# One core, two transformer blocks in three-pass matmuls: row statistics by token, eight weight slots, all weight splits on GpSimd

## The reference, cut to what matters

```
h = x
h += rms(gmlp(rms(h)))                       # u * (W_s layernorm(v) + b), gelu
h += rms(relu(rms(h) @ up)**2 @ down)        # feed-forward 1, 4096 hidden
h += rms(band_attention(rms(h), rms(h)@wk, rms(h)@wv))   # 16 heads
h += rms(relu(rms(h) @ up)**2 @ down)        # feed-forward 2
h += 0.5 * (silu(rms(h) @ gate) * (rms(h) @ up)) @ down  # feed-forward 3, 2816 hidden
h += w_out(branch_a * sigmoid + branch_b * sigmoid)      # top-k attention, retention
h += 0.5 * swiglu(rms(h))                    # feed-forward 4
h += sigmoid(rms(h) @ g) * (p @ w)           # last projection
out = rms(h)
rms(x) = x * rsqrt(mean(x*x, last axis) + eps) * gain
```

## Time and profile before

| | |
|---|---|
| median of 3 runs | 2698.27 us (2697.91 to 2699.78) |
| the profiled execution | 2702.41 us, its span 2700.6 us |
| PE busy, mean granted clock | 2487.4 us (92%), 0.944 |
| DVE, ACT, POOL busy | 1434.4, 796.1, 518.7 us |
| the chain that ended last | PE 81%, DVE 14%, ACT 2% |
| low parts by DVE (L1128), by POOL (L319) | 292 and 119 units |

### The profile page before, as it was taken

The page is one execution under the profiler, slowest core; times in us unless marked ns, Lnnn a source line. Parts: engine busy times, 40 slices in busy tenths (PEclk is TensorE's granted clock), DMA queues, the critical chain, the costliest instruction groups (busy, mean ns, idle before and its releaser), DMA issues.

```text
span 2700.6 us, 30486 instructions
## 1 busy us (share of the span) xinstructions
PE 2487.4 (92%) x10766; PEld 1964.8 (73%) x10766; DVE 1434.4 (53%) x1974; ACT 796.1 (29%) x1226; POOL 518.7 (19%) x243
## 2 busy tenths in 40 slices
PE   6888999979998999996999997978989998999996
PEld 5666888856666788884888885555567887888875
DVE  4566434473666543457534466797434336444456
ACT  2134223331433332233323232312322113322233
POOL 6600000015432000000000005452026871000000
PEclk9889999989998999997999998986599999999998
DMA  4222333322222233321333332121012323333322
GB/s 165 70 78 63 94 101 94 93 71 85 84 62 63 86 94 100 94 82 55 109 95 100 95 88 75 48 77 32 0 43 74 100 87 94 101 96 99 88 76 70
DMA packets 64805, 221.52 MB, mean 82 GB/s; under 512 B 7504, under 2 KB 9680, under 8 KB 64592
## 3 DMA queue, kind: packets, MB, share of 16 engines
q1 hardware_dynamic: 59184, 208.17, 26.0%
q10 hardware_dynamic: 5536, 12.19, 1.4%
HBM read 218.23 MB, written 2.10 MB: 82 GB/s over the span
## 4 chain that ended last, share of the span: by engine, by line
PE 81%; DVE 14%; ACT 2%; issue 2%; ACTq 0%; POOL 0%; DVEq 0%; POOLq 0%
PE PS L368 23%; PE PS L370 22%; PE PS L369 22%; PE PS L438 3%; DVE RI L1158 1%; PE PS L498 1%; PE PS L519 1%; DVE SS L1140 1%; DVE MK L1494 1%; DVE TOP L1493 1%; DVE XL L1148 1%; PE PS L708 1%; PE PS L625 1%; PE PS L646 1%; PE PS L635 1%
## 5 line engine op out<-in xcount | busy, mean ns | idle before, releaser
L368 PE MATMUL PS<-XH,WH 128*128 128x512 f32 x1816 | 730.3, 402 | 80.8 <-DVE WL L1128 35.6
L369 PE MATMUL PS<-XL,WH 128*128 128x512 f32 x1816 | 715.8, 394 | 0.0
L370 PE MATMUL PS<-XH,WL 128*128 128x512 f32 x1816 | 715.4, 394 | 0.0
L316 POOL TENSOR_TENSOR WH<-RAW,ONES 128x1024 fp32r<-128x1024 f32 (+1 forms) x119 | 231.0, 1942 | 1709.5 <-PE PS L370 1157.5
L368 PEld LDWEIGHTS PS<-XH,WH 128*128 128x128 f32 x1816 | 347.3, 191 | 182.4 <-issue 69.0
L1128 DVE TENSOR_TENSOR WL<-RAW,WH 128x1024 fp32r<-128x1024 f32 (+2 forms) x292 | 346.9, 1188 | 202.3 <-ACT WH L797 194.0
L370 PEld LDWEIGHTS PS<-XH,WL 128*128 128x128 f32 x1816 | 346.2, 191 | 73.9
L369 PEld LDWEIGHTS PS<-XL,WH 128*128 128x128 f32 x1816 | 347.3, 191 | 70.8 <-issue 1.4
L797 ACT ACTIVATE WH<-RAW 128x1024 fp32r<-128x1024 f32 (+2 forms) x292 | 297.8, 1020 | 340.2 <-DVE M L1240 336.2
L368 PE MATMUL PS<-HH,WH 128*128 128x512 f32 x992 | 389.6, 393 | 3.0 <-DVE WL L1128 3.0
L370 PE MATMUL PS<-HH,WL 128*128 128x512 f32 x992 | 386.8, 390 | 0.0
(11 more groups left out here) (202 smaller groups left out, 2412.1 us busy)
## 6 DMA issues: line engine op xcount, KB each, us to landing
RAW<-in_weights SPq DMA_DIRECT2D x379, 512.0 KB, 3.5
RAW<-in_weights SPq DMA_DIRECT2D x16, 384.0 KB, 3.1
H<-in_xT ACTq DMA_DIRECT2D x8, 256.0 KB, 8.9
BIAS<-in_rel ACTq DMA_DIRECT2D x8, 256.0 KB, 3.5
RAW<-in_weights SPq DMA_DIRECT2D x8, 256.0 KB, 2.6
out<-R ACTq DMA_DIRECT2D x8, 256.0 KB, 2.2
BIAS<-in_rel ACTq DMA_DIRECT2D x8, 224.0 KB, 3.8
DECAY<-in_decay ACTq DMA_DIRECT2D x1, 1024.0 KB, 4.9
```

The source lines that it names most:

```text
L316: nc.gpsimd.tensor_tensor(WH[:, slot, 0:w], raw, ONES[:, 0:1].to_broadcast([P, w]), ALU.mult).then_inc(high_split, 1)
L368: nc.tensor.matmul(PS[:, bank_, :], WH[:, slot, w], xh[:, k, :], start=(k == 0), stop=False)
L369: nc.tensor.matmul(PS[:, bank_, :], WH[:, slot, w], xl[:, k, :], start=False, stop=False)
L370: return nc.tensor.matmul(PS[:, bank_, :], WL[:, slot, w], xh[:, k, :], start=False, stop=stop)
```

## The change

1. **Statistics by token** everywhere: `stat` makes four matmuls with one column (SS as the stationary side), so that each token's sum is one number on a partition; root and reciprocal are over 128x4. `spread` multiplies the reciprocal, broadcast along 128 columns, by the identity, four matmuls, and so puts it back in all rows, in bank 4 (read there by L1254 instead of RI) or in bank 5, from where ACT copies it into RI.
2. **Eight weight slots** in three ranges (WIDE: units 24 to 91, 120 to 255, 331 on): WH2/WL2 (and WHA, WLA where those are in use) beside WH/WL. RAW keeps four.
3. **Four units together** at the start of a feed-forward, and the unit after them (SPARE: 28, 124, 188, 331) goes into bank 7, so it waits for no evacuation.
4. **No memset** of M: the first down group copies, the later ones add. The `ffn` code is partly unrolled for it.
5. **The rotation tables** (sines, by DVE and ACT) move from the branch of ffn_a1 into the first down group of ffn_b1.
6. **POOL splits all units**; `split_high` and `split_low` do nothing any more.

```diff
-POOL_RANGES = ((0, FIRST["gmlp_out"] + 4), (FIRST["att_v"] + 4, FIRST["ffn_a1"]),
-               (FIRST["mix_heads"] + 4, FIRST["ffn_b2"]))
+POOL_RANGES = ((0, UNITS),)
+AHEAD = 8
+WIDE = ((24, 92, 20), (120, 256, 116), (331, UNITS, 328))
+SPARE = (28, 124, 188, 331)
+def weight_slot(u):
+    for first, end, zero in WIDE:
+        if first <= u < end:
+            return (u - zero) % (2 * SLOTS)
+    return u % SLOTS
+def slot_before(u):
+    return next((v for v in range(u - 1, max(-1, u - 3 * SLOTS), -1) if weight_slot(v) == weight_slot(u)
+                 and (weight_slot(u) < SLOTS or u - v == 2 * SLOTS)), None)
+def bank_of(u):
+    return 7 if u in SPARE else u % SLOTS
...
-        ANG = at("ANG", 32, [P, 3, SEQ])
+        ANG = at("ANG", 196, [P, 2, SEQ])
...
+        WH2 = at("WH2", 144, [P, SLOTS, UNIT], F32R)
+        WL2 = at("WL2", 160, [P, SLOTS, UNIT], F32R)
+        WLA = at("WLA", 80, [P, SLOTS, UNIT], F32R)
+        WHA = at("WHA", 188, [P, 3, UNIT], F32R)
...
+        def weights_of(u):
+            k = weight_slot(u)
+            if k < SLOTS:
+                return WH[:, k, :], WL[:, k, :]
+            high = WHA[:, k - SLOTS, :] if 331 < u < 335 else WH2[:, k - SLOTS, :]
+            low = WLA[:, k - SLOTS, :] if 120 <= u < 124 else WL2[:, k - SLOTS, :]
+            return high, low
...
-                for s in range(n):
-                    slot, w = (u + s) % SLOTS, widths[u + s]
-                    pool.wait_ge(landed[slot], 16 * ((u + s) // SLOTS + 1) + step * 16)
-                    pool.wait_ge(units_done, u + s + 1 + step * SLOTS)
-                    raw = RAW[:, slot, 0:w]
-                    nc.gpsimd.tensor_tensor(WH[:, slot, 0:w], raw, ONES[:, 0:1].to_broadcast([P, w]),
+                for v in range(u, u + n):
+                    w = widths[v]
+                    raw = RAW[:, v % SLOTS, 0:w]
+                    high, low = weights_of(v)
+                    pool.wait_ge(landed[v % SLOTS], 16 * (v // SLOTS + 1) + step * 16)
+                    if v == 24:
+                        pool.wait_ge(x_ready, 2 * DT)
+                    elif v == 120:
+                        pool.wait_ge(x_done, 2 * DT * TT)
+                    elif v == 332:
+                        pool.wait_ge(units_done, FIRST["mix_out"] + SLOTS)
+                    elif slot_before(v) is not None:
+                        pool.wait_ge(units_done, slot_before(v) + 1 + SLOTS + step * SLOTS)
+                    nc.gpsimd.tensor_tensor(high[:, 0:w], raw, ONES[:, 0:1].to_broadcast([P, w]),
                                             ALU.mult).then_inc(high_split, 1)
-                    pool.wait_ge(high_split, u + s + 1 + step * SLOTS)
-                    nc.gpsimd.tensor_tensor(WL[:, slot, 0:w], raw, WH[:, slot, 0:w].bitcast(F32),
+                    pool.wait_ge(high_split, v + 1 + step * SLOTS)
+                    nc.gpsimd.tensor_tensor(low[:, 0:w], raw, high[:, 0:w].bitcast(F32),
                                             ALU.subtract).then_inc(weights_split, 1)
...
-                slot = split.n % SLOTS
+                u = split.n - SLOTS
                 pe.wait_ge(weights_split, split.next())
-                pe.wait_ge(evacuated, bank.next())
+                if u in SPARE:
+                    bank.next()
+                else:
+                    pe.wait_ge(evacuated, bank.next())
...
                     w = slice(k * P, k * P + P)
-                    last = three_passes(slot, slot, w, xh, xl, k, k == tiles - 1)
...
-            def stat(token_major=False):
+            def stat():
                 pe.wait_ge(ss_ready, ss.next(DT))
-                if token_major:
-                    for j in range(TT):
-                        nc.tensor.matmul(PS[:, 5, j:j + 1], SS[:, j * P:j * P + P], ONES[:, 0:1],
-                                         start=True, stop=True)
-                nc.tensor.matmul(PS[:, 4, :], ONES[:], SS[:], start=True, stop=True).then_inc(stat_ready, 1)
+                for j in range(TT):
+                    last = nc.tensor.matmul(PS[:, 6, j:j + 1], SS[:, j * P:j * P + P], ONES[:, 0:1],
+                                            start=True, stop=True)
+                last.then_inc(stat_ready, 1)
+            def spread(bank_):
+                pe.wait_ge(ri_ready, ri.next())
+                for j in range(TT):
+                    last = nc.tensor.matmul(PS[:, bank_, j * P:j * P + P],
+                                            RT[:, TT + j:TT + j + 1].to_broadcast([P, P]), IDENT[:],
+                                            start=True, stop=True)
+                last.then_inc(spread_ready, 1)
+            def stat_and_spread():
+                stat()
+                spread(4)
...
                 def group(size, first=False):
                     if first:
-                        together(*[(DT, XH, XL, xr)] * 3, before_last=stat)
+                        together(*[(DT, XH, XL, xr)] * SLOTS, before_last=stat)
+                        spread(5)
+                    for s in range(SLOTS if first else 0, size * ups):
                         product(DT, XH, XL)
-                    with loop(pe, size * ups // 4 - first, [(split, 4), (bank, 4)]):
-                        for s in range(4):
-                            product(DT, XH, XL)
                     hr.next(size)
                     together(*[(size, HH, HL, hr)] * 2)
-                    for s in range(6):
...
                 group(DT, first=True)
                 with loop(pe, len(sizes) - 2, [(split, per), (bank, per), (hr, DT)]):
...
-            def stat(token_major=False):
+                    split_high(first + t + AHEAD)
+            def root():
                 act.wait_ge(stat_ready, sr.next())
-                if token_major:
-                    S.activation(RT[:, 0:4], PS[:, 5, 0:4], ACT.Sqrt, bias=col(C_EPS6), scale=1.0 / D)\
-                     .then_inc(root_ready, 1)
-                S.activation(RI[:], PS[:, 4, :], ACT.Sqrt, bias=col(C_EPS6), scale=1.0 / D).then_inc(root_ready, 1)
-            def ffn(first, tiles, gated):
+                S.activation(RT[:, 0:TT], PS[:, 6, 0:TT], ACT.Sqrt, bias=col(C_EPS6), scale=1.0 / D)\
+                 .then_inc(root_ready, 1)
+            def copy_rinv():
+                act.wait_ge(spread_ready, sp_.next())
+                S.activation(RI[:], PS[:, 5, :], ACT.Copy).then_inc(ri_copied, 1)
+            def norm_rows():
+                root()
+                copy_rinv()
+            def branch_root():
+                root()
+                sp_.next()
...
+                def down_units(u, turn, tables=False):
+                    for s in range(DT):
+                        act.wait_ge(evacuated, ev.next())
+                        if tables and s < 4:
+                            act.wait_ge(to_act, ta.next())
+                            S.activation(ROT[:, (1, 0, 3, 2)[s], :], ANG[:, 0, :], ACT.Sin).then_inc(act_out, 1)
+                        split_high(u + s + AHEAD, turn)
...
+            act.wait_ge(units_done, FIRST["att_v"] + SLOTS + SLOTS)
...
-            def rinv(token_major=False):
-                if token_major:
-                    dve.wait_ge(root_ready, rr.next())
-                    V.reciprocal(RT[:, 4:8], RT[:, 0:4]).then_inc(ri_ready, 1)
-                    ri.next()
+            def recip():
                 dve.wait_ge(root_ready, rr.next())
-                V.reciprocal(RI[:], RI[:]).then_inc(ri_ready, 1)
+                V.reciprocal(RT[:, TT:2 * TT], RT[:, 0:TT]).then_inc(ri_ready, 1)
                 dve.wait_ge(ri_ready, ri.next())
+            def branch_rinv():
+                recip()
+                dve.wait_ge(spread_ready, sp_.next())
+            def rinv():
+                recip()
+                sp_.next()
+                dve.wait_ge(ri_copied, rc.next())
             def x_parts(g):
...
                         z = T[:, 2 + t % 2, :]
-                        link(V.tensor_tensor(z, m[:, t, :], RI[:], ALU.mult))
+                        link(V.tensor_tensor(z, m[:, t, :], PS[:, 4, :], ALU.mult))
                         V.scalar_tensor_tensor(H[:, t, :], z, gain(g_out, t), H[:, t, :],
...
-                V.memset(M[:], 0.0).then_inc(dve_self, 1)
-                dve.wait_ge(dve_self, me.next())
+                        low(s, 2)
+                        split_low(u + 2 * s + 1 + AHEAD, turn)
+                def down_units(u, turn, added, tables=False):
+                    for s in range(DT):
+                        src = unit()
+                        if added:
+                            V.tensor_tensor(M[:, s, :], src, M[:, s, :], ALU.add).then_inc(evacuated, 1)
+                        else:
+                            V.tensor_copy(M[:, s, :], src).then_inc(evacuated, 1)
+                        if tables and s < 5:
+                            rotation_tables(s)
+                        split_low(u + s + AHEAD, turn)
+                up = gated_units if gated else plain_units
```

(23 more changed lines are left out.)

225 lines of the change are left out of this document (107 added, 118 removed).

## The result

The changed kernel takes 2737.5 us (median of 4 runs, 2735.3 to 2737.95) against 2699.03 (4 runs): the ratio is 1.0142, 95% interval 1.0125 to 1.0158. It is slower by 1.4%, where 2675 was forecast. Its profiled execution has a span of 2735.7 us against 2700.6, 35.1 more.

The account below looks back on a forecast made before the run. PE, busy 92% of the span, was taken to lose its time at seams between stages, waiting for DVE, then at lower clock. Terms 2-12+3-8-2+4-8-2 = -23 gave 2679.4 profiled, 2675 us median; 8 in 10 range 2642 to 2708.

Parts of the forecast that it names:

- the stretches outside the seams: Steady feed-forward stages and scoring loop: nothing won or lost, the time lying at the seams between stages.
- Alternation of DVE and POOL: First two feed-forward seams: one two-operand DVE operation per POOL operation, norm tiles 7.6 us instead of 2.63; +2 and +3.
- The first down groups: First two feed-forward stages: no cost of their own; +2 and +3 were to cover each stage to its second up group.
- Tables: Third feed-forward: leaving the branch gives -7.5, standing in the first down group stalls 11 us; with the seam -8 together.
- The clean seam: Third feed-forward: POOL is done soon after PE's last unit, so the seam gains the full -2.5 and -9.5.
- V and attention: Seam after the first feed-forward: PE's waits on POOL's splits go, 6.2, 2.5 for statistics and 3.4: -12.
- statistics: Branch seams: smaller root and reciprocal, less spread (1.2 us) and copy, make each seam 2.5 to 3 us shorter.
- Fourth seam: Fourth feed-forward: POOL splits units 327 to 330 late, PE waits 1 to 2 us for unit 331: +4.
- Last projection and end: Last projection: PE's wait of 5.52 and slow clock of 2.6 go, -8; shorter statistics at the end, -2.
- Rival B: The four feed-forward stages' 264 units: POOL becomes the bound, at 5.6 us a unit costing 42: 2717, slower; chance 14%.
- Rival D: Spare bank or eight slots don't act; gains of 9.5 at three seams become 5: 2684, still faster; chance 8%.

Follow-up runs that it names:

- e1: Changed kernel with 56 extra 512-column matmuls, their results unused, filling PE's 13.96 us wait before the scoring loop: 2694.14 us, ratio to before 0.9985.
- e4: Changed kernel with POOL splitting only units 0 to 31, 92 to 127 and 256 to 334, ACT and DVE the others: 2716.75 us, ratio 1.0069.
- e7: e1 with 28 extra matmuls instead of 56, so part of the wait before the scoring loop stays empty: 2734.91 us.
- e8: e1 with 8 extra matmuls instead of 56, so most of the wait before the scoring loop stays empty: 2735.33 us.
- e11: e5 without the spare bank: four executions at 2667.91 to 2671.08 us, six at 2707.86 to 2714.79, median 2707.96.
- e13: Changed kernel with 6 extra matmuls behind the empty wait, at the start of the scoring loop: 2696.68 us, ratio to before 0.9996.
- e12: Kernel before with 9 matmuls in its 2.19 us pause ahead of the last product before the scoring loop: 2698.28 us, ratio 1.0000.
- e15: Kernel before with POOL splitting all 411 units, still four slots: 2715.24 us, ratio 1.0064.
- e9: e5 with POOL held back at the first two feed-forward seams and hand-over at units 36 and 132: 2656.61 us, ratio to before 0.9848.
- e14: e9 with three units together instead of four in the fourth feed-forward stage only: 2645.83 us, ratio to before 0.9808.
- e5: e4 with the 56 matmuls of e1 and POOL's last range reaching to unit 342 instead of 334: 2667.35 us, ratio to before 0.9884.

## Why the prediction was wrong

- **The step that failed** is one that the prediction didn't have: the stretches outside the seams were put at nothing ("Nothing is won there. The time lies at the seams between stages"), the scoring loop among them, with no reason why its clock should stay as it was. The loop lost 41.0 us with the same matmuls, 40.1 of them where PE has no wait; the filled wait gave 43.4 back (e1). Without it the profiled span would be 2694.7 against 2677 forecast. No rival of mine, B least of all, had this mechanism.
- **Why this loop.** Shown: in every profiled execution it takes 50.7 to 52.1 us from the first score matmul to the last, or 91.2 to 91.5, at the upper or the lower level nearly throughout. From 5.8 us into the loop to its last score matmul none changes its level. Where it stayed low (the changed kernel, e4, e7, e8, e11), the clock rose only 4.3 to 4.7 us behind the start of the last score matmul, in the 512-column matmuls that follow. Six dense matmuls at its head lift it (e13). Open: why the kernel before, e12 and e15, which entered as cold as the changed kernel, e4, e7 and e8, rose 3.9 to 4.3 us into the loop and by their times did so in every execution, and these in none. Up to 3.6 us into the loop, PE's rows of before and after are the same to 0.01 us. The length of the wait (7.7 to 14 us) and the short pause ahead of it are ruled out. A rival that no run was built for is that nothing in the kernel decides but the moment at which it comes to the loop; for it speaks that e11 fell in either group with the same instructions. That the change caused the low level, rather than met it, is not shown.
- **Alternation of DVE and POOL: right.** Tiles of 7.8 us against 7.6, until POOL's backlog ended at 217.7; +1.0 and +2.3 up to the first down group against +2 and +3. Released, the tiles take 2.65 (e9).
- **The first down groups: missed, +5.9 and +6.0.** I priced the seam up to unit five and took the up group for steady. But DVE starts it four evacuations late and has one slow operation in each unit. e4, with that operation at 0.69, brings 5.9 down to 1.6.
- **Tables: right,** in the wait and in size: +12.6 against 11, -19.8 against -18.5 for the seam and the branch. The clean seam itself, from the sum to the first down group, gained 10.8 of the 12 forecast. In e4, without POOL, the tables cost nothing there.
- **V and attention: -9.3 against -12;** the two waits of the earlier trace rows for POOL are gone as forecast, but statistics save 1.6 at a seam, not 2.5 to 3, as the spread is 2.08 us long instead of 1.2 and the sum hardly shorter (1.87 against 2.08), and PE has a new wait of 3.60 us (at 611.49) for V's first evacuation.
- **Fourth seam: +5.5 against +4,** for the reason given (late splits of units 327 to 331). With three units together e14 takes it away.
- **Last projection and end: -1.5 against -10.** I had let the norm's slow tiles cancel against the removed split, but PE waits 4.67 us (at 2657.56) for DVE's half step, whose operations stand beside POOL's. e5 and e4 give the forecast value with POOL gone.
- **Rival B** named the right side, slower, by luck: its mechanism was wrong. Inside the feed-forward stages the changed kernel keeps before's pace to 0.01 us.
- **Rival D's** sum is wrong: 4.5 us less at three seams is 13.5, so 2688, not 2684. It changes no side.
- Apart from the loop, the two large misses (10.3 in the down groups, 8.5 at the end) are the same one, POOL's share: priced where DVE has its norm tiles, not where it evacuates and makes the half step. That the 2.7 at V are POOL's is not shown: e4, where POOL splits from unit 92 on as well, gains 9.5 there against the changed kernel's 9.3. For POOL's share e15 finds 16.9 us net in the old structure, e4 22.8 in the new one up to the loop.
